# A two-layer hybrid encoder trunk on one core: last FFN group, decay sums, output projection and gate tiles put in another order

## The chip, the cores and the metric

The kernel runs on one core of a Trainium2 chip. The metric is the device time of one execution in microseconds (us); the kernel before takes 2820.43 us, the median of 3 runs (2819.46 to 2824.1).

## What is computed

Two layers over 1024 tokens of width 1024, all in float32. Each layer is

```python
h = rmsnorm(x, mix_norm_gain)
xbc, z, dt_raw, gu, gv, q, k, v = split(h @ w_in)
y = concat([ssd_mixer(xbc, z, dt_raw), gmlp_mixer(gu, gv), attn_mixer(q, k, v)])
x = x + y @ w_out
x = x + (silu(gate) * val) @ w_down     # gate, val = split(dwconv3(rmsnorm(x) @ w_up) + b)
```

`ssd_mixer` is a bidirectional Mamba-2 scan in 8 chunks of 128 tokens with 8 heads of 64, two B/C groups and state 128. Inside a chunk it needs, for each of 2 directions and 8 heads, the matrix exp(acs[t] - acs[s]) over the token pairs of the chunk, where acs is the running sum of dt*a. `attn_mixer` has 4 heads of 64 over three dilated windows, merged; `gmlp_mixer` mixes the 128 positions of a chunk. The FFN is 2816 wide.

## The kernel before

Each engine has one program; semaphores order them. Everything is transposed: X, the residual stream, is [128 features, 8 feature tiles, 1024 tokens], and so are HH and HL, the high and low part of the activation for which a float32 product is made of three `fp32r` matmuls (`mm3`, lines 448, 451, 452; `tokens_part`, lines 518, 521, 522). Weights stream in units of 256 columns: SyncE loads a half unit into RAW, GpSimd splits it into WH and WL (lines 437, 439), and there are two slots, so a unit is split when the unit two ahead of it has been used up (`w_used`).

A layer goes through these stages, in program order on TensorE (PE):

- The norm and the units for keys, queries and values (`keys_unit`). In layer 0 the loads of x (four of 1 MB) are queued before the first weight unit.
- Sixteen tiles of x/B/C (`columns_tile`, 8 products of three matmuls of 512 columns), with the convolution on VectorE (DVE) and small work between tiles, among it `decays`, which sums dt*a.
- Attention, `STEPS` = 32 steps (8 token tiles x 4 heads). Step j on PE is one tile of z/gu/gv (`tokens_tile`, 24 matmuls of 256 columns), `scores(j + 1)`, `turn(j)` (8 transposes), `values(j - 1)`, `fold_head(j - 2)`. DVE adds the bias (`logits`), ScalarE (ACT) takes `exps` and copies the transposed probabilities, DVE makes their low part. ACT also empties the tile (`dense_out`), and after every fourth step applies `gate`; gates 6 and 7 also take four sums of squares.
- The backward states of the scan (8 steps of `ra_turn`, `ra_state`); after step 3 DVE makes the constants IDR and FAR (`far`).
- Eight chunks (`chunk`). The sums (`sums`, four for a chunk) put acs, broadcast over partitions, and a large negative number outside the triangle, into a PSUM bank: one matmul of 512 columns with FAR (line 769) and for each of 4 heads one of 128 columns of a triangle with a broadcast column of AST (line 774; each shows as two in the trace). ACT copies AST for each chunk (line 1153).
- The y stage: `normalise` on DVE, then for each chunk 8 transposes on PE (line 844), a high part on ACT and a low part on DVE (line 1638).
- The output projection: 16 tiles of 8 products in the order `W_ORDER` (feature tile dt, token half th), DVE adding each to X (line 1655). X has been overwritten in between and comes back from memory by one load of 4 MB, issued after the last transpose.
- The norm for the FFN: the sums of squares of a token half are collected in ACC (line 1238), `norm_spread` (line 465) sums over partitions, DVE and ACT make the inverse root, `norm_back` (line 473) spreads it, DVE scales (HF, line 1253) and makes HL (line 1259), ACT makes HH. `first_unit` works through half 0 feature tile by feature tile and calls `norm_spread` and `norm_back` of half 1 on the way.
- `NG` = 11 FFN groups. PE does `up(g, part 0)` (4 tiles), `down(g - 1)` (16 tiles of 6 matmuls), `up(g, part 1)`; ACT and DVE make AHI/ALO (one buffer) from the up tiles, in loops over g with register indices. `down(10)` comes last.

The output is stored by one transfer of 4 MB after the last addition.

Of the kernel before, what the change touches and what calls it, by code (L numbers as in the profile page):

```python
# [25 lines left out]
P = 128  # L26
# [12 lines left out]
UC = 256  # L39
# [9 lines left out]
STEPS = NT * AH_  # L49
A_XBC = QKV_U * NT  # L50
# [7 lines left out]
W_ORDER = [(dt, th) for dt in range(4) for th in range(2)] + [(dt, th) for th in range(2) for dt in range(4, KT)]  # L58
# [60 lines left out]
def trunk(nc, xT, wst, params, consts, onehot, lnrow, table, outT):  # L119
# [10 lines left out]
    with ExitStack() as ctx:  # L130
# [15 lines left out]
        CST = place("CST", [P, 4 * P])  # L146
# [29 lines left out]
        ident, tri_f, tri_b, ones = (CST[:, i * P:(i + 1) * P] for i in range(4))  # L176

# [48 lines left out]
        AST = place("AST", [P, 16], u_at + 19968)  # L226
# [3 lines left out]
        AHI = place("AHI", [P, 2, SEQ], u_at, F32R)  # L230
        ALO = place("ALO", [P, 2, SEQ], u_at + 8192, F32R)
# [24 lines left out]
        GT = work("GT", [P, GW])  # L256

# [15 lines left out]
        x_spilled, x_back, y_out = sem("x_spilled"), sem("x_back"), sem("y_out")  # L273
# [15 lines left out]
        ast_ready, t_full, bst_ready, xs_ready = sem("ast_ready"), sem("t_full"), sem("bst_ready"), sem("xs_ready")  # L289
# [45 lines left out]
        def _(sp):  # L335
# [34 lines left out]
            for l in range(DEPTH):  # L370
                if l == 0:
                    weights(l, 0, 4)
# [71 lines left out]
        def _(pe):  # L444
# [50 lines left out]
            def first_unit(l, u, s, n0, n):  # L495
# [70 lines left out]
            for l in range(DEPTH):  # L566
# [64 lines left out]
                between = {0: dt_columns, 1: lambda: heads_turn(3), 2: dt_turn, 6: decays}  # L631
# [56 lines left out]
                scores(0)  # L688
                for j in range(STEPS):
# [1122 lines left out]
```

## Time and profile before

| | before |
|---|---|
| median of 3 runs | 2820.43 us (2819.46 to 2824.1) |
| the profiled execution's own time | 2819.14 us |
| its span, first to last instruction | 2817.4 us |
| PE busy | 2667.3 us, 95% of the span |
| DVE, ACT, GpSimd busy | 52%, 33%, 26% |
| mean granted TensorE clock | 0.981 of full |

What lies around the span in the profiled execution is 1.7 us. The page's lines say for each group of instructions how long the engine had stood idle before them and what ended that wait. A line of the timeline is: start, duration, engine, source line, operation, out<-in, shape, count, and in brackets the idle time before it and its releaser. An x8 row is eight instructions merged; the duration is then from the first's start to the last's end. A matmul's duration is longer than the distance to the next one's start, since matmuls overlap.

### The profile page before, as it was taken

What the parts mean: (1) busy time and instruction counts of PE and PEld (TensorE: products, weight loads), DVE (VectorE), ACT (ScalarE), POOL (GpSimd) and SP (SyncE); (2) the same over time, 40 slices, a digit from 0 to 9 for tenths busy, and PEclk for the clock granted to TensorE, in tenths of its full rate; (3) what the DMA queues carried; (4) which work ended last, traced back from release to release, by engine and by line L of the source; (5) the groups of instructions that cost most, each with busy time, mean ns of one, the idle gap of its engine ahead of it and who ended that gap; (6) DMA issues with size and microseconds to landing.
All of it is one profiled execution on the core that took longest, in us unless ns stands there. A gap on an engine that the chain in (4) does not pass through costs nothing.

```text
span 2817.4 us, 35461 instructions
## 1 busy us (share of the span) xinstructions
PE 2667.3 (95%) x13860; PEld 2241.6 (80%) x13860; DVE 1478.6 (52%) x1751; ACT 930.6 (33%) x1454; POOL 720.9 (26%) x388
## 2 busy tenths in 40 slices
PE   5999998899999999999899999898999999999997
PEld 5988987787888888888688799786878888888885
DVE  5366557826444444444465655586464444444443
ACT  3345554513222222222234355453132222222221
POOL 2232110023333333333223301100333333333330
PEclk9999999999999999999999999999999999999998
DMA  5433343121111111111123344521111111111111
GB/s 184 135 99 120 127 146 132 53 75 45 45 45 45 45 48 50 53 45 45 58 90 85 103 129 142 172 83 68 45 45 45 45 45 48 51 52 45 45 45 60
DMA packets 74104, 214.08 MB, mean 76 GB/s; under 512 B 5832, under 2 KB 30408, under 8 KB 72776
## 3 DMA queue, kind: packets, MB, share of 16 engines
q1 hardware_dynamic: 53192, 180.67, 19.9%
q10 hardware_dynamic: 20776, 31.39, 3.3%
q8 instruction: 110, 1.80, 0.3%
q14 instruction: 26, 0.21, 0.0%
HBM read 178.45 MB, written 33.59 MB: 75 GB/s over the span
## 4 chain that ended last, share of the span: by engine, by line
PE 89%; DVE 6%; ACT 2%; issue 2%; DMA 0%; ACTq 0%; DVEq 0%; SPq 0%
PE PS L448 22%; PE PS L451 22%; PE PS L452 21%; PE PS L518 4%; PE PS L522 3%; PE PS L521 3%; PE PS L774 2%; PE PS L672 2%; PE PS L661 2%; PE PS L790 1%; PE PS L651 1%; PE PS L650 1%; PE PS L824 1%; DVE ACC L1238 1%; DVE HL L1259 1%
## 5 line engine op out<-in xcount | busy, mean ns | idle before, releaser
L448 PE MATMUL PS<-HH,WH 128*128 128x512 f32 x1920 | 765.4, 399 | 4.7 <-DVE HL L1638 4.7
L451 PE MATMUL PS<-HL,WH 128*128 128x512 f32 x1920 | 763.6, 398 | 0.0
L452 PE MATMUL PS<-HH,WL 128*128 128x512 f32 x1920 | 763.3, 398 | 0.0
L437 POOL CAST WH<-RAW 128x1024 fp32r<-128x1024 f32 x192 | 235.0, 1224 | 2019.3 <-PE PS L448 1526.5
L439 POOL TENSOR_TENSOR WL<-RAW,WH 128x1024 fp32r<-128x1024 f32 x192 | 491.4, 2559 | 15.4
L1655 DVE TENSOR_TENSOR X<-PS,X 128x512 f32<-128x512 f32 x384 | 259.7, 690 | 398.8 <-PE PS L452 378.5
L448 PEld LDWEIGHTS PS<-HH,WH 128*128 128x128 f32 x1920 | 363.2, 189 | 93.5 <-DVE HL L1638 5.2
L452 PEld LDWEIGHTS PS<-HH,WL 128*128 128x128 f32 x1920 | 363.2, 189 | 88.8
L451 PEld LDWEIGHTS PS<-HL,WH 128*128 128x128 f32 x1920 | 363.4, 189 | 88.0
L1197 ACT ACTIVATE FPAD<-PS 128x512 f32<-128x512 f32 x176 | 103.2, 600 | 886.9 <-PE PS L452 886.7
L1674 DVE SCALAR_TENSOR_TENSOR CVV<-FPAD,PARM,CVV 128x1024 f32<-128x1024 f32 x44 | 87.1, 1980 | 415.8 <-ACT CVV L1203 415.8
L448 PE MATMUL PS<-AHI,WH 128*128 128x512 f32 x704 | 281.4, 400 | 17.4 <-issue 17.4
L451 PE MATMUL PS<-ALO,WH 128*128 128x512 f32 x704 | 280.9, 399 | 0.0
L452 PE MATMUL PS<-AHI,WL 128*128 128x512 f32 x704 | 280.5, 398 | 0.0
L518 PE MATMUL PS<-WH,HH 128*128 128x256 f32 x896 | 263.8, 294 | 16.4 <-DVE HL L1259 9.0
L521 PE MATMUL PS<-WL,HH 128*128 128x256 f32 x896 | 255.8, 285 | 0.0
L522 PE MATMUL PS<-WH,HL 128*128 128x256 f32 x896 | 255.4, 285 | 0.0
L518 PEld LDWEIGHTS PS<-WH,HH 128*128 128x128 f32 x896 | 172.1, 192 | 19.3 <-DVE HL L1259 8.3
L448 PEld LDWEIGHTS PS<-AHI,WH 128*128 128x128 f32 x704 | 133.7, 190 | 50.8 <-issue 18.2
L521 PEld LDWEIGHTS PS<-WL,HH 128*128 128x128 f32 x896 | 173.2, 193 | 0.1
L522 PEld LDWEIGHTS PS<-WH,HL 128*128 128x128 f32 x896 | 172.9, 193 | 0.0
L452 PEld LDWEIGHTS PS<-AHI,WL 128*128 128x128 f32 x704 | 133.7, 190 | 32.7
(199 smaller groups left out, 3234.8 us busy)
## 6 DMA issues: line engine op xcount, KB each, us to landing
RAW<-wst SPq DMA_DIRECT2D x192, 512.0 KB, 3.5
TOE<-toe_d SPq DMA_DIRECT2D x64, 512.0 KB, 3.7
XBS<-xbc_d SPq DMA_DIRECT2D x24, 512.0 KB, 4.4
xspill<-X ACTq DMA_DIRECT2D x2, 4096.0 KB, 13.0
xbc_d<-CV ACTq DMA_DIRECT2D x16, 512.0 KB, 3.4
tok_d<-ST ACTq DMA_DIRECT2D x16, 512.0 KB, 3.2
ZG<-tok_d SPq DMA_DIRECT2D x16, 512.0 KB, 3.5
X<-xspill SPq DMA_DIRECT2D x2, 4096.0 KB, 12.1
```

The costliest lines, as they stand in the source:

```text
L437: nc.gpsimd.tensor_copy(hi, RAW[:, hf, :]).then_inc(hi_done, 1)
L439: nc.gpsimd.tensor_tensor(WL[:, s, hf * 1024:(hf + 1) * 1024], RAW[:, hf, :], hi.bitcast(F32), ALU.subtract).then_inc(w_ready, 1)
L448: ins = nc.tensor.matmul(out, wh, xh, start=first, stop=False)
L451: nc.tensor.matmul(out, wh, xl, start=False, stop=False)
L452: return nc.tensor.matmul(out, wl, xh, start=False, stop=last)
L518: ins = nc.tensor.matmul(o, xh, WH[:, s, cols], start=(k == 0), stop=False)
L521: nc.tensor.matmul(o, xh, WL[:, s, cols], start=False, stop=False)
L522: return nc.tensor.matmul(o, xl, WH[:, s, cols], start=False, stop=(k == KT - 1))
L661: last = nc.tensor.transpose(PS[:, 4 + t // 4, (t % 4) * P:(t % 4 + 1) * P], LG[:, j % 2, t * P:(t + 1) * P], ident)
L1197: A(FPAD[:, x % 2, 1 + th * HALF:1 + (th + 1) * HALF], bank(f % 4), ACT.Copy).then_inc(a_free, 1)
L1655: TT(x, bank(4 + i % 4), x, ALU.add).then_inc(b_free, 1)
L1674: step.then(STT(t, FPAD[:, x % 2, 0:SEQ], PARM[:, bass.ds(g * 8 + at, 1)], t, ALU.mult, ALU.add))
```

## The change

- The order of the last FFN group: `up(10, part 0)`, `up(10, part 1)`, `down(9)`, `down(10)`. AHI and ALO have two buffers, by the parity of g. DVE's work of the last group is written out with the additions of `down(9)` between its steps. The loops over g on ACT and DVE are unrolled, with constant indices in place of register ones.
- The decay sums: `decays_turn` transposes all of acs once for a layer, into the place of the parameter `w_dt`; `far` also makes SEL and, from the transposed rows, MH and ML (high and low part, each row in one of 4 blocks of 128 columns). A sum is then the FAR matmul and two of 512 columns, SEL's broadcast column with MH and with ML. AST and its copy are gone.
- The output projection: `W_ORDER` takes feature tiles 0 to 3 for half 0, then for half 1, then 4 to 7 likewise. It begins after the low parts of chunks 0 to 3; the transposes of chunks 4 to 7 follow its first two tiles. X comes back in two loads of 2 MB, after the transposes of chunk 5 and of chunk 7.
- The gate tiles run two ahead of their step (`LEAD` = 2): three before `scores(1)`, none in steps 30 and 31; `gate(7)` follows `evac(29)`.
- The FFN norm: addition 15 comes one tile of scaling and two of low parts sooner; `norm_spread` and `norm_back` of half 1 stand before feature tiles 4 and 6, where they stood before 2 and 5.
- The start: the first weight unit is queued after two of the four loads of x.
- The end: the output goes out as 2 MB (half 0), 1 MB and 1 MB.

```diff
--- before.py
+++ after.py
+LEAD = 2
...
-W_ORDER = [(dt, th) for dt in range(4) for th in range(2)] + [(dt, th) for th in range(2) for dt in range(4, KT)]
+W_ORDER = [(dt, th) for part in range(2) for th in range(2) for dt in range(part * 4, part * 4 + 4)]
...
-        AHI = place("AHI", [P, 2, SEQ], u_at, F32R)
-        ALO = place("ALO", [P, 2, SEQ], u_at + 8192, F32R)
+        AHI = [place(f"AHI{i}", [P, 2, SEQ], u_at + i * 40992, F32R) for i in range(2)]
+        ALO = [place(f"ALO{i}", [P, 2, SEQ], u_at + 8192 + i * 40992, F32R) for i in range(2)]
...
+        MH = place("MH", [P, 4, P], m_at[0], F32R)
+        ML = place("ML", [P, 4, P], m_at[0] + 2048, F32R)
...
+                if i == 2:
+                    weights(0, 0, 1)
...
-                sp.wait_ge(yn_ready, (l + 1) * NT)
-                sp.wait_ge(yt_full, 2 + (l + 1) * NT)
-                sp.dma_start(X[:], xspill[:, :, :]).then_inc(x_back, 16)
+                for part in range(2):
+                    sp.wait_ge(yn_ready, l * NT + 6 + 2 * part)
+                    sp.wait_ge(yt_full, 2 + l * NT + 6 + 2 * part)
+                    k = slice(part * 4, part * 4 + 4)
+                    sp.dma_start(X[:, k], xspill[:, k]).then_inc(x_back[part], 16)
                 weights(l, 14, UNITS)
-            sp.wait_ge(b_free, BF + 4 + DEPTH * B_FILLS)
-            sp.dma_start(outT[:, :, :], X[:]).then_inc(y_out, 16)
-            sp.wait_ge(y_out, 16)
+            for th, k in ((0, slice(0, KT)), (1, slice(0, 4)), (1, slice(4, KT))):
+                sp.wait_ge(b_free, BF + 4 + DEPTH * B_FILLS - 16 + KT * th + k.stop)
+                sp.dma_start(outT[:, k, half(th)], X[:, k, half(th)]).then_inc(y_out, 16)
+            sp.wait_ge(y_out, 48)
...
-                        if th == 0 and k == 2:
+                        if th == 0 and k == 4:
                             norm_spread(n, 1)
-                        if th == 0 and k == 5:
+                        if th == 0 and k == 6:
...
+                def decays_turn():
+
+                    pe.wait_ge(acs_ready, l + 1)
+                    nc.tensor.transpose(PS[:, 4, 0:P], ACS[:].rearrange("p c e -> p (c e)"), ident).then_inc(acst_full, 1)
+
+                between = {0: dt_columns, 1: lambda: heads_turn(3), 2: dt_turn, 6: decays, 8: decays_turn}
...
+                def gates(j):
                     u, t = QKV_U + XBC_U + j // NT, j % NT
                     if t == 0:
                         unit_ready(l, u)
                     tokens_tile(a0, A_TOK + j, u, t)
+
+                scores(0)
+                for j in range(LEAD):
+                    gates(j)
+                for j in range(STEPS):
+                    if j + LEAD < STEPS:
+                        gates(j + LEAD)
...
-                        if j == 0:
-                            pe.wait_ge(ast_ready, n + 1)
                         pe.wait_ge(exp_ready, n * 4 + j + 1)
                         nc.tensor.matmul(bank(2 + j % 2), IDR[:, :],
                                          FAR[:, d, :].unsqueeze(1).to_broadcast((P, 4, P)),
                                          start=True, stop=False, skip_group_check=True)
-                        for h in range(4):
-                            e = d * 8 + g * 4 + h
-                            last = nc.tensor.matmul(PS[:, 2 + j % 2, h * P:(h + 1) * P],
-                                                    AST[:, e:e + 1].to_broadcast((P, P)),
-                                                    tri_f if d == 0 else tri_b, start=False, stop=True,
-                                                    skip_group_check=True)
+                        rows = n % NT * 4 + d * 2 + g
+                        for part in (MH, ML):
+                            last = nc.tensor.matmul(bank(2 + j % 2), SEL[:, rows:rows + 1].to_broadcast((P, P)),
+                                                    part[:].rearrange("p h n -> p (h n)"), start=False,
+                                                    stop=part is ML, skip_group_check=True)
...
-                pe.wait_ge(yz_ready, 2 + (l + 1) * NT)
-                for c in range(NT):
+                def y_turn(c):
...
-                pe.wait_ge(yl_ready, 2 + (l + 1) * NT)
+                for c in range(4):
+                    y_turn(c)
                 n = 2 * l + 1
                 for i, (dt, th) in enumerate(W_ORDER):
                     u, ct = divmod(dt, 2)
                     s = (IN_U + u) % SLOTS
                     if (ct, th) == (0, 0):
                         unit_ready(l, IN_U + u)
+                    if i in (0, 4):
+                        pe.wait_ge(yl_ready, 2 + l * NT + 4 + i)
                     pe.wait_ge(b_free, BF + b0 + i + 1)
-                    follows = i in (4, 8, 14)
+                    follows = i in (6, 8, 14)
                     at, between = {12: (4, norm_spread), 13: (4, norm_back)}.get(i, (None, None))
                     columns_tile(u, s, ct, th, 4 + i % 4, follows, at, between and (lambda: between(n, 0))
                                  ).then_inc(b_full, 1)
+                    if i < 2:
+                        y_turn(4 + 2 * i)
+                        y_turn(5 + 2 * i)
...
-                for g in range(1, NG):
+                for g in range(1, NG - 1):
                     u = f0 + 3 * g - 1
                     up(g, u, u % SLOTS, 0)
                     down(g - 1, u + 1, (u + 1) % SLOTS)
                     up(g, u + 2, u % SLOTS, 1)
+                for part in range(2):
+                    up(NG - 1, UNITS - 4 + part, (UNITS + part) % SLOTS, part)
+                down(NG - 2, UNITS - 2, UNITS % SLOTS)
                 down(NG - 1, UNITS - 1, (UNITS - 1) % SLOTS, l + 1 < DEPTH)
...
-                high_norm(n, 0, 5, KT)
+                high_norm(n, 0, 5, 7)
                 squares(n, b_value, 15, 16)
+                high_norm(n, 0, 7, KT)
...
                 exps(0)
+                for j in range(LEAD):
+                    dense_out(j)
                 for j in range(STEPS):
-                    dense_out(j)
+                    if j + LEAD < STEPS:
+                        dense_out(j + LEAD)
                     if j + 1 < STEPS:
                         exps(j + 1)
                     evac(j)
                     if j == 0:
                         silu_out(7)
-                    if j % 4 == 3:
-                        gate(j // 4)
+                    if (j + LEAD) % 4 == 3 and j + LEAD < STEPS:
...
-                    act.wait_ge(ab_full, 1 + n * 4)
-                    A(AST[:], DTA[:, c, :], ACT.Copy).then_inc(ast_ready, 1)
...
-                scale_on(n, 0, 6, KT + 1)
+                scale_on(n, 0, 6, 7)
                 add(15)
+                scale_on(n, 0, 7, KT)
                 total(n, 15)
+                scale_on(n, 0, KT, KT + 1)
...
+                dve.wait_ge(acst_full, l + 1)
+                nc.vector.tensor_copy(par_("w_dt"), PS[:, 4, 0:P])
...
-                        last = TS(FAR[:, d, :], tri, 1.0, 1e30, ALU.subtract, ALU.mult)
+                        TS(FAR[:, d, :], tri, 1.0, 1e30, ALU.subtract, ALU.mult)
+                    nc.vector.tensor_copy(SEL[:], fours)
+                    for h in range(4):
+                        last = TS(MH[:, h, :], par_("w_dt"), fourth[:, h:h + 1], None, ALU.mult)
+                    last.then_inc(far_step, 1)
+                    dve.wait_ge(far_step, l + 1)
+                    for h in range(4):
+                        last = STT(ML[:, h, :], par_("w_dt"), fourth[:, h:h + 1], MH[:, h, :].bitcast(F32),
+                                   ALU.mult, ALU.subtract)
...
+                g, n0 = NG - 1, b0 + B_FILLS - 32
+                step.begin(l * NG + g)
+                for x in range(3):
+                    conv(g, x)
+                add(0, n0)
+                conv_first(g, 3)
+                low(g, 0)
+                add(1, n0)
+                conv_last(g, 3)
+                for i in range(2, 4):
+                    add(i, n0)
+                gated(g, 1)
+                for i in range(4, 6):
+                    add(i, n0)
+                low(g, 1)
+                step.end()
+                for i in range(6, 16):
+                    add(i, n0)
```

## Rows read from the trace of the kernel before

**Rows 1.** Waits of PE: waited for, us in total, times, longest us

```profile
PE PS L448 <- issue: 17.4, 2, 8.7
```

**Rows 2.** Timeline of PE and DVE in the last `down` of layer 1

```profile
2779.62 0.77 PE L448 MATMUL PS<-AHI,WH 128*128 128x512 f32 x1 [8.71 <-issue]
...
2789.69 0.69 DVE L1655 TENSOR_TENSOR X<-PS,X 128x512 f32<-128x512 f32 x1 [0.71 <-PE PS L452]
...
2805.15 0.69 DVE L1655 TENSOR_TENSOR X<-PS,X 128x512 f32<-128x512 f32 x1 [0.71 <-PE PS L452]
```

**Rows 3.** DMA issues: count, KB each, median us to landing

```profile
RAW<-wst SPq DMA_DIRECT2D x192, 512.0 KB, 3.5
...
outT<-X SPq DMA_DIRECT2D x1, 4096.0 KB, 11.1
```

**Rows 4.** Timeline of DVE and PE in the FFN norm of layer 0

```profile
644.40 0.68 DVE L1259 TENSOR_TENSOR HL<-HF,HH 128x512 fp32r<-128x512 f32 x1
...
658.57 3.63 DVE L1259 TENSOR_TENSOR HL<-HF,HH 128x512 fp32r<-128x512 f32 x2
...
663.50 1.45 DVE L1238 TENSOR_TENSOR ACC<-ACC,SQ 128x512 f32<-128x512 f32 x1 [0.70 <-ACT SQ L909]
...
665.01 1.87 PE L465 MATMUL PS<-CST,ACC 128*128 128x2 f32 x8 [6.50 <-DVE ACC L1238]
```

**Rows 5.** Windows: length, busy of PE, PEld, DVE, ACT, POOL; PEclk, DMA

```profile
449.11:530.71 81.60, 77.34 (x576) 72.87 (x575) 70.28 (x115) 46.56 (x166) 0.00 (x0) 1.00 0.24 78
424.60:445.00 20.40, 12.74 (x68) 9.72 (x68) 14.63 (x28) 3.91 (x10) 0.00 (x0) 1.00 0.64 237
...
655.70:679.10 23.40, 16.90 (x65) 13.65 (x65) 12.91 (x17) 4.75 (x10) 8.16 (x4) 0.78 0.14 46
```

**Rows 6.** Timeline of PE and DVE in the second chunk of layer 0

```profile
462.15 0.58 PE L769 MATMUL PS<-FAR,IDR 128*128 128x512 f32 x1
...
463.37 0.47 PE L769 MATMUL PS<-FAR,IDR 128*128 128x512 f32 x1
...
466.19 1.10 PE L808 MATMUL PS<-XW,BC 128*128 128x256 f32 x4 [0.61 <-DVE GT L1592]
...
465.62 0.42 DVE L1592 TENSOR_TENSOR GT<-PS,PARM 128x256 f32<-128x256 f32 x1 [0.21 <-PE PS L798]
...
472.48 0.69 DVE L1617 TENSOR_TENSOR Y<-Y,PS 128x512 f32<-128x512 f32 x1 [0.68 <-PE PS L824]
```

**Rows 7.** Timeline of DVE in the backward states of layer 0

```profile
434.74 0.36 DVE L1529 TENSOR_SCALAR FAR<-CST 128x128 fp32r<-128x128 f32 x2
435.01 0.68 DVE L1541 TENSOR_TENSOR XWA<-PS,WST 128x512 f32<-128x512 f32 x1
```

**Rows 8.** Timeline of DVE and PE from the y stage into the projection

```profile
553.21 1.23 DVE L1638 TENSOR_TENSOR HL<-PS,HH 128x1024 fp32r<-128x1024 f32 x1 [0.41 <-ACT HH L1180]
...
558.34 0.44 PE L844 MATMUL PS<-CST,YT 128*128 128x128 f32 x2 [0.48 <-DVE HL L1638]
...
562.16 0.51 PE L448 MATMUL PS<-HH,WH 128*128 128x512 f32 x1 [2.37 <-DVE HL L1638]
```

**Rows 9.** Timeline of PE in attention, layer 0

```profile
232.43 0.80 PE L650 MATMUL PS<-KX,QH 128*128 128x512 f32 x1 [5.49 <-DVE MN L1453]
...
391.05 1.03 PE L661 MATMUL PS<-CST,LG 128*128 128x128 f32 x8
...
404.92 1.06 PE L661 MATMUL PS<-CST,LG 128*128 128x128 f32 x8 [2.03 <-DVE PTX L1460]
...
416.02 1.06 PE L661 MATMUL PS<-CST,LG 128*128 128x128 f32 x8
```

**Rows 10.** Timeline of PE, GpSimd and DVE at the start

```profile
28.19 0.58 PE L518 MATMUL PS<-WH,HH 128*128 128x256 f32 x1 [7.39 <-POOL WL L439]
...
20.46 1.04 POOL L437 CAST WH<-RAW 128x1024 fp32r<-128x1024 f32 x1 [20.01 <-DMA RAW<-wst]
...
28.61 5.75 DVE L1238 TENSOR_TENSOR ACC<-ACC,SQ 128x512 f32<-128x512 f32 x3
```

More of the change, by code:

```diff
@@ L145, in trunk @@
         PARM = place("PARM", [P, NPAR])
-        CST = place("CST", [P, 4 * P])
+        CST = place("CST", [P, 4 * P + 36])
         QSL = place("QSL", [P, AH_, P], top[0], F32R)
@@ L225, in trunk @@
         FAR = place("FAR", [P, 2, P], u_at + 18944, F32R)
-        AST = place("AST", [P, 16], u_at + 19968)
+        SEL = place("SEL", [P, 32], u_at + 19968, F32R)
         XBS = place("XBS", [P, 2, XBC_T, P], u_at + 49184)
         XBR = place("XBR", [P, 2, XBC_T, P], u_at)
-        AHI = place("AHI", [P, 2, SEQ], u_at, F32R)
-        ALO = place("ALO", [P, 2, SEQ], u_at + 8192, F32R)
+        AHI = [place(f"AHI{i}", [P, 2, SEQ], u_at + i * 40992, F32R) for i in range(2)]
+        ALO = [place(f"ALO{i}", [P, 2, SEQ], u_at + 8192 + i * 40992, F32R) for i in range(2)]
         FPAD = place("FPAD", [P, 2, SEQ + 2], u_at + 16384)
@@ L371, in _ @@
                 if l == 0:
-                    weights(l, 0, 4)
+                    weights(l, 1, 4)
                     sp.wait_ge(row_sb, 1)
@@ L1128, in _ @@
                         silu_out(7)
-                    if j % 4 == 3:
-                        gate(j // 4)
+                    if (j + LEAD) % 4 == 3 and j + LEAD < STEPS:
+                        gate((j + LEAD) // 4)
                 for i in range(NT):
@@ L1184, in _ @@
                 ffn_norm(2 * l + 1, 4 + b0 + BF)
-                settle(act)
-                with act.Fori(0, NG) as g:
+                for g in range(NG):
                     n = l * NG + g
@@ L1212, in high @@
                         act.wait_ge(f_conv, 1 + n * 4 + 3 + ct)
-                        if ct == 0:
-                            act.wait_ge(b_full, b0 + 4 * OUT_U + g * 16)
-                        A(AHI[:, ct, :], CVV[:, ct, :], ACT.Copy).then_inc(f_hi, 1)
+                        if ct == 0 and g >= 2:
+                            act.wait_ge(b_full, b0 + 4 * OUT_U + (g - 1) * 16)
+                        A(AHI[g % 2][:, ct, :], CVV[:, ct, :], ACT.Copy).then_inc(f_hi, 1)
                     take(0)
@@ L1666, in _, with conv_first @@
                 step = Steps(dve, f_step, 6)
-                def conv(g, x):
+                def conv_first(g, x):
                     part, ct = divmod(x, 2)
-                    n = l * NG + g
                     t = (CVG, CVV)[part][:, ct, :]
-                    at = PAR["ffn_conv"][0] + (part * FT + ct) * 4
-                    dve.wait_ge(f_tap, n * 4 + x + 1)
-                    step.then(STT(t, FPAD[:, x % 2, 0:SEQ], PARM[:, bass.ds(g * 8 + at, 1)], t, ALU.mult, ALU.add))
-                    ins = STT(t, FPAD[:, x % 2, 2:2 + SEQ], PARM[:, bass.ds(g * 8 + at + 2, 1)], t,
-                              ALU.mult, ALU.add)
+                    at = PAR["ffn_conv"][0] + (part * FT + ct) * 4 + g * 8
+                    dve.wait_ge(f_tap, (l * NG + g) * 4 + x + 1)
+                    step.then(STT(t, FPAD[:, x % 2, 0:SEQ], PARM[:, at:at + 1], t, ALU.mult, ALU.add))
@@ L1677, in conv, with conv_last @@
+                def conv_last(g, x):
+                    part, ct = divmod(x, 2)
+                    t = (CVG, CVV)[part][:, ct, :]
+                    at = PAR["ffn_conv"][0] + (part * FT + ct) * 4 + g * 8
+                    ins = STT(t, FPAD[:, x % 2, 2:2 + SEQ], PARM[:, at + 2:at + 3], t, ALU.mult, ALU.add)
                     if part:
                         step.then(ins)
-                        dve.wait_ge(f_silu, n * 2 + ct + 1)
-                        ins = TT(t, t, CVG[:, ct, :], ALU.mult)
@@ L1687, in low, with conv @@
                        ).then_inc(act_ready, 1)
-                def group(g, adds):
+                def conv(g, x):
+                    conv_first(g, x)
+                    conv_last(g, x)
+                    if x >= 2:
+                        gated(g, x - 2)
+                for g in range(NG - 1):
                     step.begin(l * NG + g)
@@ L1692, in group @@
                     conv(g, 0)
-                    for f in range(4 if adds else 0):
-                        add(f, n0)
+                    for i in range(4 if g else 0):
+                        add(i, n0)
                     conv(g, 1)
-                    for f in range(4, 16 if adds else 4):
-                        add(f, n0)
+                    for i in range(4, 16 if g else 4):
+                        add(i, n0)
                     conv(g, 2)
@@ L1702, in group @@
                     step.end()
-                group(0, False)
-                settle(dve)
-                with dve.Fori(1, NG) as g:
-                    group(g, True)
+                g, n0 = NG - 1, b0 + B_FILLS - 32
[11 more added lines that the diff above has]
+                for i in range(4, 6):
+                    add(i, n0)
+                low(g, 1)
+                step.end()
+                for i in range(6, 16):
+                    add(i, n0)
                 n0 = b0 + B_FILLS - 16
@@ L1758, in weight_stream @@
             units += [cols(w_up[l], g * UC)]
-            if g:
+            if 0 < g < NG - 1:
                 units += [rows(w_down[l], (g - 1) * UC)]
             units += [cols(w_up[l], FFN + g * UC)]
-        units += [rows(w_down[l], (NG - 1) * UC)]
+        units += [rows(w_down[l], g * UC) for g in (NG - 2, NG - 1)]
     return np.stack(units)
```

36 lines of the change are left out of this document (21 added, 15 removed).

## The prediction

> **What bounds the kernel now.** PE is busy for 95% of the span and at full clock for 98% of it, and no matmul of the large products is taken away. So the change can only win back time in which PE stands idle, and time in which it runs at 1.2 instead of 2.4 GHz after it has stood idle. I read the waits of PE first, then the timeline around each, then the other engines there. The longest waits of one kind are those of the last `down`: twice 8.7 us [rows 1]. The reader should see in each place what stands behind the wait: 8.71 us before `down(10)`, and additions 1.40 us apart once it runs at 2.4 GHz, so 0.234 us for each of a tile's six matmuls [rows 2]; 11.1 us for the output after everything is computed [rows 3]; a wait of 6.50 us for ACC in the FFN norm, with the granted clock at 0.78 over the stretch around it [rows 4, 5]; a chunk in which both PE and DVE are nearly always busy [rows 5, 6]; backward states in which DVE goes from FAR straight to the next XWA [rows 7]; 2.37 us before the projection, for DVE's low parts [rows 8]; 5.49 us in attention's second step [rows 9]; and 7.39 us for the first weights [rows 10].
>
> **The last FFN group.** PE stops at 2770.9 (2779.62 less 8.71), and its last tile is added from 2805.15 on [rows 2]. Sixteen tiles of 1.405 are 22.5 us; the stretch is 34.2, so 11.7 are lost: 8.7 idle and 3.0 at the low clock. In the new order `down(9)`, 22.5 us of work with its inputs long made, lies between the last up tile and `down(10)`. The chain that took 8.7 must now share DVE with six additions of 0.69: about 13 us, hidden by 22.5. If that cover were gone, what exceeds it would be PE's wait again. Additions wait behind convolution and low parts on DVE, and PE behind the additions only after four banks (5.6 us); I take no wait, at most 2. Gain 11.7 a layer, 23.4 in all (19 to 24). Unrolling the loops on ACT and DVE touches no path here: PE has no waits inside the groups. I take 0.
>
> **The FFN norm.** Half 0 of `first_unit` lasts from 655.7 to 679.1 [rows 5]. Its work is eight feature tiles of six matmuls (11.2 us) and two norm steps of about 1.0, 13.2 us; 10.2 are lost, 6.5 idle [rows 4] and 3.7 at the low clock. Now PE has four tiles (until 661.3) before it asks for ACC, not two. On DVE, addition 15 can run at 657.9, where a scaling ran, then the scaling (until 659.2), one low part, then ACC's last sum. The low part takes 0.68 alone and 1.8 (3.63 for two) here, where GpSimd splits a unit; the sum 1.45 [rows 4]. That gives 660.6 to 662.5, so PE idles 0 to 1.2 us and, I take it, keeps its clock: gain 9 a layer, 18 in all. With the low clock as before and 1.2 idle it is 5.3 a layer, the other bound (10.5 to 20).
>
> The rows show a DVE instruction with two SBUF sources stretched from 0.68 to 1.8 while GpSimd works. The Trainium skill ("GPSIMD Engine Reference", Specifications) says that GpSimd shares its SBUF interfaces with VectorE and contends with VectorE instructions that have two SBUF inputs. By that rule both the low part and the sum stay stretched after they are moved, which gives the late end, 662.5; without it the sum would come out at 660.6.
>
> **The chunks.** A sum takes 1.22 us on PE (463.37 less 462.15) [rows 6]. The new one is three matmuls of 512 columns, for which the trace has no row with a broadcast column of `fp32r`. Bounds: 3 x 0.234 = 0.70 by the large products, and 3 x 0.43 = 1.28 at half clock, no gain. I take 0.79, with a tenth for the change of kind: 0.43 less, 1.7 for a chunk. PE then needs 11.66 - 0.61 - 1.7 = 9.35 (the period is 81.6/7, the wait is at line 808) [rows 5, 6]. DVE needs 11.66 - 0.21 - 0.68 = 10.77 [rows 6]. So DVE bounds the stage: six periods lose 0.89 each, the first chunk, where DVE only follows PE, loses 1.7 and 0.7, the last 0.2. Gain 7.9 a layer, 15.8 in all (8 to 19). AST's copy was off both paths.
>
> Against it stands `far`: two instructions of 128 columns take 0.27 before the next XWA can start [rows 7]. Four more of that kind are 0.55, SEL and a wait 0.15, four with two sources (a quarter of 0.68 each) 0.7: 1.4 us on DVE, in a stage where PE waits for DVE, PE being busy 12.74 of 20.4 us [rows 5]. Cost 1.4 a layer, 2.8 in all (2 to 6). The transpose of acs adds about 0.3 to PE a layer, 0.6. DVE waits for it behind `conv5(2)`, where it would have stood idle until the next tile is tapped; at most 1 a layer.
>
> **The projection.** The low part of chunk 3 ends at 554.4, the projection began at 562.16 [rows 8]: 7.7 us sooner. But the transposes of chunks 4 to 7, which ran under DVE's work, now stand between tiles: eight of them take some 1.1 (558.34 and on, without the wait inside) [rows 8], so 4.4 come back. Gain 3.3 a layer, 6.6 in all (2 to 9). X's first 2 MB (6.7 us, interpolated in [rows 3]) leave at about 562 and are due when PE wants its fifth bank, at 581: hidden, by 12 us. Weights 14 and on are queued behind the second load, at some 570; PE wants them 60 us later.
>
> **The gate tiles.** DVE is late here because of the last convolution, not of PE: turn 1 starts when it does, whatever PE has done. So the 5.49 us are filled with two tiles, but nothing behind them starts sooner; 29 steps follow with the same work on PE, and the tiles are missing in steps 30 and 31. There the chain over DVE and ACT sets the pace. Turns 29 to 31 take 11.1 us now (404.92 to 416.02) with gate 7 after them. Two turns with such a gate between take 13.87 (391.05 to 404.92) [rows 9], and gate 7 now falls there: 13.4 without a tile to copy, 2.3 us more. PE idles some 6 us in it, and after 8.7 idle the low clock cost 3.0 [rows 2]; I take 1.7. Cost 4 a layer, 8 in all. Bounds: 6 a layer lost, and 5.5 a layer won if the hole does not come back (-11 to +12).
>
> **The start and the end.** The first unit comes after 2 MB of x and not 4 MB, about 6 us sooner than 20.46 [rows 10]. Norm and low parts, not weights, then hold PE, from 23 on instead of 28.19; and the second unit's split no longer stretches DVE's three sums, 5.75 us for what takes about 2 [rows 10]. Gain 5 (0 to 7.4). At the end 1 MB is left: by the line through 3.5 us for 0.5 MB and 11.1 for 4 MB it takes 4.6 [rows 3], 6.5 less (5 to 7.6).
>
> **The sum.** -23.4 - 18 - 15.8 + 2.8 + 0.6 - 6.6 + 8 - 5 - 6.5 = -63.9. From the profiled execution's own 2819.14 that is 2755.2; the median of the runs lies 1.3 above it: 2756.5 us.
>
> **The rivals.**
>
> *The tiles ahead pay.* If the steps had slack that PE could use, the 5.49 us would stay won, in place of 4 lost: 9.5 a layer, 2737.5 us. For it: the wait is the longest in attention. Against it: turn 1 hangs on DVE and ACT. 12%.
>
> *The norm keeps its wait.* The moved sum is stretched, PE falls to 1.2 GHz as before: 3.7 a layer lost, and with `far` or attention at their dear ends 2764 to 2779 us. For it: 3.63 us for two low parts [rows 4]. This is where the skill's rule of the shared interfaces, which the trace agrees with, leads. 15%.
>
> *The last group does not hide its chain.* DVE, with additions between the steps of the convolution, is late for `down(10)` or for the banks; if all of it stayed, 2780 us. Against it: 13 us in 22.5. 5%.
>
> *The chunk stage falls to 1.2 GHz.* PE is busy 77.34 of 81.6 us there now, and would be 9.35 of 10.77. At half clock it needs 9.35 x 0.43/0.234 = 17.1 a chunk, 6.4 over DVE's, 16 times: 2858 us, slower than before. From 70% of the stage at the low clock on, it eats all the gain (64/16 = 4 a chunk). Against it: the backward states keep a clock of 1.00 with PE busy 62% [rows 5]. 3%.
>
> The Trainium skill ("TensorE: Matmul & The Clock Gate", Part 1) has it that the throttled state is the default and activity lifts it, so a thinner stage could fall back; by that rule, were it to bite at 87%, the time is that of this rival. The trace speaks against it here.
>
> **How the numbers follow.** My forecast, 2756.5 us, has 63%; its own range is 2745 to 2768. The rivals have 12, 15, 5 and 3%, no measurable change 2%. Leaving out the lower part of the first rival and the last two cases, the range is 2740 to 2779. A change of 0.2% (5.6 us) is about what a measurement can tell from none. Faster by more 95%, within it 2%, slower 3%.
>
> **What would show it.** Right: no wait before the last `down`; L465 waiting under 1.5 us in the FFN norm; chunks 10.8 us apart, with DVE idle under 0.3 in each; the projection's first tile some 2 us after chunk 3's transposes, and no wait of PE before its fifth; turn 31 of attention about 13.4 after turn 29; the last transfer under 5 us. Wrong: a clock below 1.00 among the chunks, banks waited for in `down(9)`, or attention shorter than before.

## The result and the profile after

The changed kernel takes 2738.05 us (median of four runs, 2735.88 to 2741.96) against 2819.94 us: a ratio of 0.971 (0.969 to 0.973). The forecast was 2756.5 us with a range of 2740 to 2779. The direction was right, the time lies below the range. The profiled execution went from 2819.14 to 2739.92 us, 79.2 less, where the sum had 63.9.

The waits of PE in the changed kernel, as in [rows 1]:

```profile
PE PS L477 <- DVE ACC L1267: 26.2, 5, 16.8
PE PS L678 <- DVE PTX L1495: 26.0, 10, 6.2
PE PS L828 <- DVE GT L1635: 20.6, 16, 1.5
...
PE PS L460 <- DVE X L1698: 4.9, 4, 1.8
PE PS L460 <- issue: 4.8, 2, 2.4
```

The wait of 8.7 us before the last `down` is gone; in its place PE waits four times, at most 1.8 us, for banks. The norm still waits for ACC (L477). Here is the last group on DVE, then PE's two bank waits and GpSimd's split beside them:

```profile
2687.47 2.96 DVE L1716 SCALAR_TENSOR_TENSOR CVV<-FPAD,PARM,CVV 128x1024 f32<-128x1024 f32 x1
2690.47 1.95 DVE L1734 TENSOR_TENSOR ALO<-CVV,AHI 128x1024 fp32r<-128x1024 f32 x1
...
2692.94 2.80 DVE L1722 SCALAR_TENSOR_TENSOR CVV<-FPAD,PARM,CVV 128x1024 f32<-128x1024 f32 x1
...
2709.44 0.69 DVE L1698 TENSOR_TENSOR X<-PS,X 128x512 f32<-128x512 f32 x1 [0.71 <-PE PS L464]
2710.84 0.69 DVE L1698 TENSOR_TENSOR X<-PS,X 128x512 f32<-128x512 f32 x1 [0.71 <-PE PS L464]
...
2717.72 0.69 DVE L1698 TENSOR_TENSOR X<-PS,X 128x512 f32<-128x512 f32 x1 [0.68 <-PE PS L464]
2719.09 0.69 DVE L1698 TENSOR_TENSOR X<-PS,X 128x512 f32<-128x512 f32 x1 [0.68 <-PE PS L464]
```

```profile
2693.07 0.50 PE L460 MATMUL PS<-AHI,WH 128*128 128x512 f32 x1 [0.65 <-DVE X L1698]
2696.52 0.50 PE L460 MATMUL PS<-AHI,WH 128*128 128x512 f32 x1 [1.79 <-DVE X L1698]
```

```profile
2691.41 3.24 POOL L451 TENSOR_TENSOR WL<-RAW,WH 128x1024 fp32r<-128x1024 f32 x1
```

Two things are to be seen. The two steps of the convolution take 2.96 and 2.80 us where the same kind takes 1.28 with GpSimd at rest, and the additions behind them, which free PE's banks, come late (that the split is the cause is tested below). And the additions of `down(9)` follow each other every 1.40 us, those of `down(10)` every 1.37, although both make PE do six matmuls and PE waits in neither. In the kernel before the step was 1.405 for `down(10)` [rows 2] and 1.407 for `down(9)`. PE has become faster, and no part of the prediction has a term for that. The projection shows it too. These are additions of one tile of 24 matmuls each, 5.62 us apart before and 5.49 after:

```profile
580.87 0.69 DVE L1655 TENSOR_TENSOR X<-PS,X 128x512 f32<-128x512 f32 x1 [4.93 <-PE PS L452]
586.49 0.69 DVE L1655 TENSOR_TENSOR X<-PS,X 128x512 f32<-128x512 f32 x1 [4.93 <-PE PS L452]
```

```profile
579.77 0.69 DVE L1698 TENSOR_TENSOR X<-PS,X 128x512 f32<-128x512 f32 x1 [4.20 <-PE PS L464]
585.26 0.69 DVE L1698 TENSOR_TENSOR X<-PS,X 128x512 f32<-128x512 f32 x1 [4.20 <-PE PS L464]
```

The spacing, the mean time from one matmul's start to the next's, comes out to four digits when it is taken over all matmuls of 512 columns that follow each other without a wait: 0.2343 us in every product before; 0.2290 after where HH or AHI0 is read, 0.2333 where AHI1 is.

The norm, DVE, then GpSimd, then PE (compare [rows 4]):

```profile
644.53 2.24 DVE L1288 TENSOR_TENSOR HL<-HF,HH 128x512 fp32r<-128x512 f32 x1
...
647.95 2.69 DVE L1288 TENSOR_TENSOR HL<-HF,HH 128x512 fp32r<-128x512 f32 x1
650.57 0.68 DVE L1267 TENSOR_TENSOR ACC<-ACC,SQ 128x512 f32<-128x512 f32 x1
```

```profile
643.49 2.74 POOL L451 TENSOR_TENSOR WL<-RAW,WH 128x1024 fp32r<-128x1024 f32 x1
...
647.75 2.34 POOL L451 TENSOR_TENSOR WL<-RAW,WH 128x1024 fp32r<-128x1024 f32 x1
```

```profile
651.30 1.86 PE L477 MATMUL PS<-CST,ACC 128*128 128x2 f32 x8 [3.82 <-DVE ACC L1267]
```

The sum comes at 650.57, right behind two low parts of 2.24 and 2.69 us; PE waits 3.82 us, and its clock falls behind that (matmuls 0.427 us apart from 653.6 to 657.4).

The backward states and the chunks by windows (the columns of [rows 5]), and what DVE puts into the states:

```profile
446.85:521.82 74.97, 65.77 (x408) 58.21 (x406) 69.22 (x115) 45.38 (x158) 0.00 (x0) 1.00 0.25 85
418.13:442.85 24.72, 15.68 (x69) 11.72 (x69) 17.05 (x38) 3.79 (x8) 0.00 (x0) 0.85 0.54 192
```

```profile
429.43 0.86 DVE L1567 TENSOR_SCALAR MH<-PARM,CST 128x128 fp32r<-128x128 f32 x4
430.32 1.14 DVE L1571 SCALAR_TENSOR_TENSOR ML<-PARM,CST,MH 128x128 fp32r<-128x128 f32 x4
431.38 0.68 DVE L1584 TENSOR_TENSOR XWA<-PS,WST 128x512 f32<-128x512 f32 x1
```

```profile
432.17 1.95 PE L741 MATMUL PS<-XWA,BSTA 128*128 128x256 f32 x4 [3.29 <-DVE XWA L1584]
```

Seven chunks take 74.97 us, 10.71 each, at a clock of 1.00. The backward states take 24.72 instead of 20.8 and 21.8 (layers 0 and 1), at a clock of 0.85. PE now waits 3.29 us for one XWA, and the state behind it runs at the low clock (1.95 instead of 1.10 us). A chunk's sum, one matmul with FAR and two with MH and ML:

```profile
454.41 0.48 PE L790 MATMUL PS<-FAR,IDR 128*128 128x512 f32 x1
454.73 0.40 PE L795 MATMUL PS<-MH,SEL 128*128 128x512 f32 x1
454.97 0.40 PE L795 MATMUL PS<-ML,SEL 128*128 128x512 f32 x1
455.20 0.40 PE L790 MATMUL PS<-FAR,IDR 128*128 128x512 f32 x1
```

Turns 29 and 31 of attention, the first and the last of the three, and the output's last transfers (1 MB in 4.3 us, where [rows 3] had 4 MB in 11.1):

```profile
394.21 1.04 PE L678 MATMUL PS<-CST,LG 128*128 128x128 f32 x8
...
407.81 1.51 PE L678 MATMUL PS<-CST,LG 128*128 128x128 f32 x6 [6.21 <-DVE PTX L1495]
```

```profile
outT<-X SPq DMA_DIRECT2D x2, 1024.0 KB, 4.3
```

### The profile page after: what moved, and what is told of

Read it like the earlier page. It is cut to its first block, busy times and chain, and to the rows that moved or that the text cites. A ratio compares the mean times of both kernels' runs of the same rounds, so it can differ in the third digit from the quotient of the medians.

```text
span 2738.1 us, 33541 instructions
## 1 busy us (share of the span) xinstructions
PE 2597.2 (95%) x13478; PEld 2199.7 (80%) x13478; DVE 1499.5 (55%) x1771; ACT 869.8 (32%) x1398; POOL 728.6 (27%) x388
## 4 chain that ended last, share of the span: by engine, by line
PE 82%; DVE 12%; ACT 4%; issue 2%; DMA 0%; ACTq 0%; DVEq 0%; SPq 0%
PE PS L460 21%; PE PS L463 21%; PE PS L464 21%; PE PS L530 3%; PE PS L533 3%; PE PS L534 3%; PE PS L689 2%; PE PS L678 2%; DVE ACC L1267 1%; DVE SEG L1646 1%; PE PS L668 1%; DVE HL L1288 1%; PE PS L667 1%; PE PS L741 1%; DVE SEG L1645 1%
## 5 line engine op out<-in xcount | busy, mean ns | idle before, releaser
L464 PE MATMUL PS<-HH,WL 128*128 128x512 f32 x1920 | 752.2, 392 | 0.0
L1716 DVE SCALAR_TENSOR_TENSOR CVV<-FPAD,PARM,CVV 128x1024 f32<-128x1024 f32 x44 | 95.4, 2167 | 377.4 <-ACT CVV L1232 377.4
```

The costliest lines, as they stand in the source:

```text
L464: return nc.tensor.matmul(out, wl, xh, start=False, stop=last)
L1716: step.then(STT(t, FPAD[:, x % 2, 0:SEQ], PARM[:, at:at + 1], t, ALU.mult, ALU.add))
```

## The experiments

Two questions were open: what made the products faster, and why the named steps gave less than the sum had. All ratios are against the kernel before, run beside on the same chip (2817.8 to 2821.6 us there). The changed kernel was not run again beside them; a difference to it compares medians from different chips and is good to about 3 us.

**Addresses.** CST has grown by 36 columns, and that moved every tile placed after it by 160 bytes. The first run does only that to the kernel before:

```diff
         CST = place("CST", [P, 4 * P])
+        GAP = place("GAP", [P, 40])
```

> The kernel before with one unused tile of 160 bytes per partition placed behind CST, as CST's 36 new columns do it in the change; nothing else. Theory A (SBUF addresses): HH and AHI then start on a multiple of 64 bytes, where they now start 32 bytes past one, and a product's matmul is issued every 0.229 us instead of every 0.234; 7872 such matmuls by 0.0054 is 42 us, and the token tiles add a few: about 2772 us. Rival B (something else of the change, such as the unrolled loops, quickens PE): the time stays at 2820 us and the spacing at 0.2343.

Measured: 2777.32 us, ratio 0.984 (0.981 to 0.987), 44 us less (36 to 52). The spacing is 0.2289 in all products, taken over the three matmuls of each. Counted, that is 42 us, and the 2688 matmuls of 256 columns came down from 0.120 to 0.116 us, 9 more. Not all of the 51 reaches the time: PE's wait for ACC in each of the two FFN norms, for one, grew from 6.5 to 8.2 us. A tile that nothing reads or writes gives over half of what the whole change gives; the unrolled loops are not in this kernel.

Two runs shift the changed kernel:

```diff
-        PARM = place("PARM", [P, NPAR])
+        PARM = place("PARM", [P, NPAR + 1])
+        QGN = PARM[:, NPAR:NPAR + 1]
...
-        QGN = place("QGN", [P, 1])
```

> The changed kernel with all tiles behind PARM 32 bytes lower, by giving QGN a free column of PARM; nothing else. Theory A: HH and AHI0 start 32 bytes past a multiple of 64, AHI1 on one. So the spacing is 0.234 for HH and AHI0 and 0.229 for AHI1, the reverse of now; 6912 matmuls by 0.0054 less 960 by 0.0044 is 33 us, some 5 to 9 more for the token tiles: 2771 to 2780 us. Rival B: 2738 us.

Measured: 2757.75 us (0.979, 0.976 to 0.981), 20 us more than the changed kernel. The reversal came as said, 0.2333 for HH and AHI0, 0.2290 for AHI1, but the time rose by less than was expected: 6912 less 960 matmuls by 0.0043 is 26 us, and the norm, measured as below, is 4.0 and 5.2 us shorter than in the changed kernel.

```diff
-        VR = place("VR", [P, NT])
+        VR = place("VR", [P, NT], top[0] - 32)
...
-        AHI = [place(f"AHI{i}", [P, 2, SEQ], u_at + i * 40992, F32R) for i in range(2)]
+        AHI = [place(f"AHI{i}", [P, 2, SEQ], u_at + i * 41024, F32R) for i in range(2)]
```

(ALO likewise, and QGN as above.)

> The changed kernel with AHI1 and ALO1 moved up by 32 bytes relative to AHI0, and all tiles behind PARM 64 bytes lower. Theory A: everything that a product reads starts on a multiple of 64; AHI1's matmuls come every 0.229 instead of 0.2333 us, 960 by 0.0044 is 4 us: about 2734 us. If not a multiple of 64 but one odd multiple is what counts (HH moves from 64 past a multiple of 128 to a multiple of 128), all spacings change. Rival B: 2738 us.

Measured: 2723.67 us (0.966, 0.964 to 0.967), 14 us less than the changed kernel, not 4. AHI1 came to 0.229 as expected, but HH and AHI0 went to 0.2267. Counted, that is 19 us; some of it is lost to the tiles of 256 columns (0.122 instead of 0.120 us a matmul). So "a multiple of 64" is not the rule. The kernel before, moved so that HH and AHI start on a multiple of 256 (the diff of the second run), should then be as fast or faster still:

> The kernel before with all tiles behind PARM 32 bytes lower (QGN in a free column of PARM): HH and AHI start on a multiple of 256. Theory A1 (what counts is a multiple of 64): the spacing is 0.229 as at an offset of 64 and 192, about 2777 us. Theory A2 (graded, as 0.2268 at an offset of 128 hints): it is 0.2268 or less, 7872 matmuls by 0.0075 is 59 us, about 2762 us or less. Rival B: 2820 us.

Measured: 2804.39 us (0.995, 0.993 to 0.996), spacing 0.2324. Both forms of the theory fell: the roundest address gives one of the slow spacings. The operation by itself, other engines idle (line 52 to 59: columns 0, 32, ... 224 bytes past a multiple of 256; line 62 to 69: the weights likewise):

```diff
+            run(both, 0, 0, 512, 4 * N)
+            for cols in (512, 256):
+                for rows in (OFFS, OFFS[::-1]):
+                    for o in rows:
+                        run(moving[o // 32], 0, o, cols, N)
+                    for o in rows:
+                        run(stationary[o // 32], o, 0, cols, N)
+            for o in (64, 96, 128, 160):
+                run(both, o, o, 512, N)
+            run(both, 0, 0, 512, N).then_inc(done, 1)
```

> A program of its own, which computes nothing of the reference and writes x back: 48 matmuls at a time of 128x128 weights and 512 columns, then of 256, fp32r, with all other engines idle. The moving operand starts 0, 32, ... 224 bytes past a multiple of 256, with the weights at 0; then the weights do, with the columns at 0; each series once up and once down. Theory A (start address): the spacing depends on the offset: least at multiples of 64, some 0.005 us more at the odd multiples of 32, if the operand's own address decides it. Rival B (what counts is how PE's operands lie to other engines' traffic or to each other only in the kernel): all 16 series have one spacing.

Its timeline; the time for 48 matmuls is the difference between two rows' starts:

```profile
60.89 11.04 PE L52 MATMUL PS<-MOV,STA 128*128 128x512 f32 x48
71.77 11.37 PE L53 MATMUL PS<-MOV,STA 128*128 128x512 f32 x48
82.97 11.16 PE L54 MATMUL PS<-MOV,STA 128*128 128x512 f32 x48
93.97 11.37 PE L55 MATMUL PS<-MOV,STA 128*128 128x512 f32 x48
105.18 11.36 PE L56 MATMUL PS<-MOV,STA 128*128 128x512 f32 x48
116.38 11.40 PE L57 MATMUL PS<-MOV,STA 128*128 128x512 f32 x48
127.62 11.35 PE L58 MATMUL PS<-MOV,STA 128*128 128x512 f32 x48
138.81 11.35 PE L59 MATMUL PS<-MOV,STA 128*128 128x512 f32 x48
150.00 11.06 PE L62 MATMUL PS<-MOV,STA 128*128 128x512 f32 x48
...
172.09 11.36 PE L64 MATMUL PS<-MOV,STA 128*128 128x512 f32 x48
183.29 11.40 PE L65 MATMUL PS<-MOV,STA 128*128 128x512 f32 x48
...
216.88 11.16 PE L68 MATMUL PS<-MOV,STA 128*128 128x512 f32 x48
227.88 11.36 PE L69 MATMUL PS<-MOV,STA 128*128 128x512 f32 x48
...
598.57 54.76 PE L50 MATMUL PS<-MOV,STA 128*128 128x512 f32 x240
```

The columns at 0, 32, 64, 96 bytes: 10.88, 11.20, 11.00, 11.21 us for 48, then 11.20, 11.24, 11.19 and 11.19. The weights at 64: 11.20, but at 192: 11.00, the mirror image. So it isn't the address of either operand but the distance, columns less weights, modulo 256: weights at 192 are a distance of 64. Taken in reverse the series repeats. The last row (`both`, line 50) is the direct test: columns and weights are moved together, by 64, 96, 128, 160 and 0 bytes, so that the distance stays 0, and the spacing stays at 0.2272 to 0.2277 us through all 240. In the kernels WH and WL start at the same place modulo 256, and every tile's step is a multiple of 256, so that each product has one distance. (The absolute addresses named in the expectations above hang on where a kernel's first tile starts, which no run shows; the distances do not.)

```
distance   alone     in a kernel (spacing, us)
0          0.2267    third run's HH, AHI0: 0.2267 to 0.2269
32         0.2334    second run's HH, AHI0: 0.2333
64         0.2291    changed kernel's HH, AHI0; first run's HH, AHI: 0.2289
96         0.2335    changed kernel's AHI1: 0.2333
128        0.2330    fourth run's HH, AHI: 0.2324
160        0.2342    kernel before's HH, AHI: 0.2343
192, 224   0.2332    -
```

Alone and in the kernels, the six distances agree within 0.0006. For 256 columns the series gives 0.113 to 0.120: 0.120 at the distances 0 and 96 in both directions, and for the others no order that both share.

**The gate tiles.**

```diff
-LEAD = 2
+LEAD = 0
```

> The changed kernel with LEAD = 0, the order of the kernel before in attention. By the prediction's theory the two tiles ahead cost 4 us a layer, so without them it is 8 us faster, 2730 us, with the 5.5 us wait back in the second step and turn 29 to 31 in about 11.1 us instead of 13.6. Rival: the steps have slack, the tiles ahead pay, and it is 2 to 11 us slower, 2740 to 2749 us.

Measured: 2730.80 us (0.968, 0.966 to 0.970), 7.3 us less than the changed kernel, as the prediction's theory had it. Its turns 29 and 31, which are 11.04 us apart instead of 13.60:

```profile
401.86 1.06 PE L678 MATMUL PS<-CST,LG 128*128 128x128 f32 x8 [2.10 <-DVE PTX L1495]
...
412.90 1.06 PE L678 MATMUL PS<-CST,LG 128*128 128x128 f32 x8 [0.17 <-DVE PTX L1495]
```

Turn 0 comes 5.65 us sooner without the tiles ahead, but turn 1 starts 18.4 us behind the last product of the x/B/C tiles in this kernel, in the changed one and in the one before, as the prediction said: it hangs on DVE. From turn 1 to turn 29 the tiles ahead then win 0.4 us (168.1 and 168.5), from turn 29 to 31 they cost 2.6, and from there to the first `ra_state` 1.6 (10.32 us, not 8.70): 3.8 to 4.0 us a layer.

**GpSimd's split.** To place the two waits, GpSimd's loop is unrolled as well.

```diff
-            with pool.Fori(0, DEPTH * UNITS // SLOTS) as r:
+            for r in range(DEPTH * UNITS // SLOTS):
...
+                            if u == IN_U + OUT_U + 1:
+                                pool.wait_ge(sq_used, (2 * l + 2) * SUMS)
+                            if u == UNITS - 1:
+                                pool.wait_ge(act_ready, 1 + (l + 1) * NG * 2)
```

> The changed kernel in which GpSimd waits at two places of a layer before it splits the next unit of weights: the second unit of the FFN until the norm's last sum (ACC) is made, and the last unit of the layer until the last low part of the last FFN group. Theory A (a DVE instruction with two SBUF sources is stretched while GpSimd splits): the two low parts before that sum take 0.68 us and not 2.24 and 2.69, so PE's wait of 3.8 us goes with the low clock behind it (2 us), 5.5 us a layer; in the last group the bank waits of 2.6 us go: in all 11 to 16 us, 2722 to 2727 us. Rival B (the low parts are late because of DVE's own order): the wait stays at 3.5 to 4 us and the time at 2738 us; and if the delayed split then holds PE up, it is slower.

Measured: 2721.75 us (0.966, 0.964 to 0.967), 16.3 us less, at the upper end of the 11 to 16 expected. DVE, and then PE:

```profile
649.50 0.68 DVE L1293 TENSOR_TENSOR HL<-HF,HH 128x512 fp32r<-128x512 f32 x1
650.10 0.68 DVE L1272 TENSOR_TENSOR ACC<-ACC,SQ 128x512 f32<-128x512 f32 x1
```

```profile
651.24 0.95 PE L482 MATMUL PS<-CST,ACC 128*128 128x2 f32 x8
```

GpSimd rests from 643.3 to 651.0 us here. The low parts are back at 0.68 us, PE doesn't wait for ACC at all, and in the last group it has no wait left (nor has its convolution a step over 1.28 us). From the first norm sum to the second `norm_back` the norm is 7.0 us a layer shorter, the FFN behind it 2.6.

**The sums.** The old sums in the changed kernel:

```diff
-                        for part in (MH, ML):
-                            last = nc.tensor.matmul(bank(2 + j % 2), SEL[:, rows:rows + 1].to_broadcast((P, P)),
+                        for h in range(4):
+                            e = d * 8 + g * 4 + h
+                            last = nc.tensor.matmul(PS[:, 2 + j % 2, h * P:(h + 1) * P],
+                                                    AST[:, e:e + 1].to_broadcast((P, P)),
```

> The changed kernel with the sums of the kernel before (ACT's copy AST and four matmuls a sum, no MH, ML, SEL, no transposed acs). By the prediction the new sums win 15.8 us in the chunks and cost 3.4 elsewhere, so without them it is 12.4 us slower: 2750 us. The trace of the changed kernel has 6.1 us a layer won in the chunks and 3.9 and 3.0 more in the backward states, which is 5.3 in all: 2743 us. Rival: the loss in the backward states isn't the sums' (another cause would stay here), 2750 us again with a backward stage as long as now.

Measured: 2748.16 us (0.975, 0.974 to 0.977), 10.1 us more in the medians and 6.1 in the profiled executions (spans of 2744.2 and 2738.1). The window of the backward states:

```profile
420.10:441.86 21.76, 14.21 (x68) 10.75 (x68) 15.06 (x29) 3.89 (x9) 0.00 (x0) 0.92 0.60 218
```

The states are 3.0 us shorter (21.76 to 24.72), the way to the first chunk's L810 0.6, and the seven periods 6.6 longer. By the traces the new sums win 3.1 a layer and by the medians 5.0, where the prediction had 6.2. The median lies nearer to the 2750 us of the rival than to 2743, but the rival's condition, a backward stage as long as now, is not met. Is the loss in the states the work itself, or its place?

```diff
                     step.end()
+                    if i >= 2:
+                        far(i - 2)
                     dve.wait_ge(ra_s_full, n + 1)
...
-                    if i == 3:
-                        far()
```

> The changed kernel with DVE's twelve preparing instructions (IDR, FAR, SEL, MH, ML) put two at a time before the additions of backward states 2 to 7, where DVE waits some 0.7 us for PE, in place of all twelve behind state 3. Theory: the 3.0 us a layer that the backward states grew, and 0.6 of a slower clock at the first chunk, come back: 7 us, 2731 us. Rival: DVE's chain sets the pace of each state, and the twelve cost the same where they are: 2738 us.

Measured: 2730.59 us (0.969, 0.967 to 0.971), 7.5 us less: the place.

```profile
419.39:440.31 20.92, 14.43 (x69) 10.62 (x69) 17.50 (x38) 3.80 (x8) 0.00 (x0) 0.91 0.63 227
```

DVE is busy as long as before (17.50 and 17.05 us), in a stage 3.8 us shorter.

**All of it together,** with AHI1 and ALO1 where they have the distance 0 too:

```diff
-        AHI = [place(f"AHI{i}", [P, 2, SEQ], u_at + i * 40992, F32R) for i in range(2)]
+        AHI = [place(f"AHI{i}", [P, 2, SEQ], u_at + i * 32768, F32R) for i in range(2)]
-        FPAD = place("FPAD", [P, 2, SEQ + 2], u_at + 16384)
+        FPAD = place("FPAD", [P, 2, SEQ + 2], u_at + 49152)
```

> The changed kernel with everything that the runs point to: HH, HL, both AHI and both ALO at the same distance of 0 modulo 256 from the weights (AHI1 and ALO1 take the place of the convolution's tiles, FPAD goes behind them), LEAD = 0, GpSimd's two splits later, and the preparation of the sums spread over the backward states. Theory: spacing 0.227 in every product; 14.4 + 1.9 us for the addresses, 7.3 for LEAD, 16.3 for the splits, 6 to 7 for the states: 2738 - 46 = 2692 us. Rival: the waits that are gone let others appear (the banks, the attention's chain), and half of the last two is lost: 2700 us or more.

Measured: 2691.29 us, ratio 0.955 (0.953 to 0.956): 46.8 us less than the changed kernel, with a spacing of 0.2267 in every product. The parts add up (14.4, 1.9, 7.3, 16.3 and 7.5 are 47.4), and nothing new takes their place. This is the fastest version.

## Why the prediction was wrong

The sum against what the traces give, both layers, the quicker products taken out of each stage (their number by 0.0053 us):

```
step of the sum          predicted   measured
last FFN group             -23.4       -17.6
FFN norm                   -18.0        -5.5
chunks                     -15.8       -13.4
far, transposed acs         +3.4        +8.0
projection                  -6.6        -4.6
gate tiles                  +8.0        +7.8
start                       -5.0        -5.0
end                         -6.5        -6.5
spacing of the matmuls       0         -42.4
sum                        -63.9       -79.2
```

The last line but one is what remains of 79.2. Counted, it is 6912 matmuls by 0.0053 and 960 by 0.001, 37.6 us, some 4 for the tiles of 256 columns ahead of attention and 2 within it, 43.6 in all.

**The step that failed** is where the prediction begins: "no matmul of the large products is taken away. So the change can only win back time in which PE stands idle" or runs slow. That holds the 0.234 us of a matmul for a constant, and it was used as one in every term. It hangs on where the operands lie, and the wider CST moved them. The edit stood in the diff, and the prediction gave it no line. The run with the unused tile and the operation by itself show it; nothing in the trace of before could have priced it, since all its products of 512 columns lie at one distance. (The same opening calls PE "at full clock for 98%" of the span. With a mean of 0.981 and half clock for the rest it is 96%; no term was made of it.)

**The FFN norm** is the second failure, and there the rival was right. The low parts were taken as 0.68 to 1.8 us; they took 2.24 and 2.69, PE waited 3.8 us and not 0 to 1.2, and the clock fell. The prediction put addition 15 at 2.2 us after the half's start and counted one low part behind it; the addition came at 4.9 us (646.70 less 641.8), because a stretched sum and a low part of 2.24 us lay ahead of it. The rows had it: 3.63 us for two [rows 4], and the rival that names GpSimd's split got 15%. "Keeps its wait" is too strong, since it fell from 6.5 to 3.8. The rule of the Trainium skill ("GPSIMD Engine Reference", Specifications) that was set beside it is borne out: with the split moved, both stretched instructions are back at 0.68 us.

**The last group** gave 17.6 and not 23.4. The order works: PE's lost time fell from 11.8 to 3.0 us a layer. "I take no wait, at most 2" was 2.6 us of bank waits, from the same stretching, since the delay of DVE was counted in instructions of their undisturbed length; 5.8 us in all.

**The chunks** went as described: DVE sets the period, 10.71 us against 10.77 predicted, a sum takes 0.70 to 0.79 us, the wait is at the old line 808 (now L828). The 2.4 us too much are the first chunk. The transposes before its sums and the first sum (1.25 us, where it was 1.13) ran at the low clock, and only the second took 0.70: the way from the first transposes to the first L810 is 4.00 us, where it was 3.40. Elsewhere the stage kept a clock of 1.00 with PE busy 65.77 of 74.97 us; the rival of the fallen clock, and the rule of the Trainium skill ("TensorE: Matmul & The Clock Gate", Part 1) that stood beside it, did not decide anything there.

**`far`** was sized at 1.4 a layer from single instructions and cost 2.0 on DVE; the other half is PE's low clock after a wait of 3.29 us and at the first chunk. The prediction had that price for other waits and left it out here.

**The projection** began 2.4 us after chunk 3's transposes, about as said, but after waits of 3.95 us before the transposes and 2.42 behind them, and at the low clock for 14 matmuls, 3.0 us.

**The gate tiles and the end** came out, **the start** in part by luck. Turn 1 came when it did before, turn 29 to 31 took 13.60 us (13.4 predicted), and the run with LEAD = 0 gives 7.3 against 8. The start is one draw: PE is through with the first weight unit at 59.2 us in the changed kernel, the earliest of all, and at 59.6 to 64.2 in its seven variants; in the kernel before at 64.8, in its two shifted ones at 63.0 and 64.9. From mean to mean that is 3 us and not 5. The last transfer took 4.3 us.

**Unrolling** was worth 0, as taken: the FFN stage of the first run, 722.2 us, less 8.8 for the last group and plus 2.1 for AHI1's slower products, is 715.5; the changed kernel has 715.4.

So by the traces the named steps gave 36.8 us, 27 less than predicted: 2782 us from 2819, beyond even the range's slow end. The first run gives a second estimate. It has the new addresses and none of the steps, and the changed kernel is 39 us below it, 43 if the 4 us of AHI1's slower products are put back: 2776 us. The steps are worth 37 to 43 us, then, and alone they end about the range's slow end of 2779. That the time came out below the fast end is luck, through an effect that was not named. It is luck too that it lies at the 2737.5 us of the first rival: that one has attention shorter, and the tiles ahead cost 7.3 us.

## What to carry to other kernels

Before pricing a change, list what it does to the addresses of every tile behind a resized one, and compare the spacing of equal matmuls before and after as the first look at two traces: it costs one division and decides how all other differences are read. An instruction of DVE that reads two SBUF sources beside a split on GpSimd may take up to four times its length (1.6 to 4.0 times here); the cure was to move the split, not the instruction. Small preparations belong where their engine waits already, and a wait of 3 us on PE is to be priced with the slow stretch behind it.

## What the runs showed of the hardware

For fp32r matmuls of 128x128 weights and 512 columns at full clock, the time from one to the next depends on the distance of the two SBUF operands' start addresses modulo 256: 0.2267 us at 0, 0.2291 at 64, 0.232 to 0.234 elsewhere, 3% between the ends, with the other engines idle as in the kernel. Moving both operands together changes nothing of it. In this kernel, with 7872 of them, one unused tile is worth 44 us (36 to 52). What it is in the memory that makes the distance count stays open.
